# Tiles 0 and 1 of layer 0 taken through the slices of x together, and four smaller reorderings, in a two-layer hybrid encoder

## What is computed

```python
def hybrid_layer(x, ...):
    h = rms_norm(x, g)
    z = h @ w_in                       # 1024 -> 3712 columns, 29 tiles of 128
    # splits: aq ak av ag | bq bk bv bg | ca cb cg
    ya = neighbourhood_attention(aq, ak, av, rpb) * silu(ag)      # 4 heads, local window 8 x 16
    yb = dilated_attention(rotary(bq), rotary(bk), bv) * silu(bg) # 6 heads, three dilated windows
    yc = conformer_conv(ca, cb, ...) * silu(cg)                   # GLU, 31 taps, LayerNorm, pointwise
    return x + concat([ya, yb, yc]) @ w_out

h = x
for l in range(2):
    h = hybrid_layer(h, ...)
return rms_norm(h, final_g)
```

## Time and profile before

| | us |
|---|---|
| median of 3 runs | 562.41 |
| lowest and highest | 561.2, 562.55 |
| profiled execution | 561.84 |
| its span (first to last instruction) | 560.0 |

### The profile page before, as it was taken

The page is one execution under the profiler, slowest core; times in us unless marked ns, Lnnn a source line. Parts: engine busy times, 40 slices in busy tenths (PEclk is TensorE's granted clock), DMA queues, the critical chain, the costliest instruction groups (busy, mean ns, idle before and its releaser), DMA issues.

```text
span 560.0 us, 7459 instructions
## 1 busy us (share of the span) xinstructions
PE 543.9 (97%) x2716; PEld 419.8 (75%) x2716; DVE 368.7 (66%) x710; ACT 248.2 (44%) x465; POOL 213.0 (38%) x251
## 2 busy tenths in 40 slices
PE   7999999999999999999899999999999999999994
PEld 5788777676776787878777876767767687878883
DVE  6799999999743644612338998999994346453113
ACT  6333255454454454623332314544555445563422
POOL 0003456544354344326211325554436434243520
PEclk9999999999999999999999999999999999999998
DMA  8724677665576674999302349756567666379913
GB/s 267 258 76 114 163 167 172 153 136 121 124 169 134 148 156 89 252 272 198 119 0 95 95 109 228 170 117 143 137 132 166 147 151 153 76 170 222 189 36 150
DMA packets 30132, 83.64 MB, mean 149 GB/s; under 512 B 4240, under 2 KB 10256, under 8 KB 30096
## 3 DMA queue, kind: packets, MB, share of 16 engines
q0 software_dynamic: 17856, 61.09, 50.1%
q1 hardware_dynamic: 12240, 22.08, 11.9%
HBM read 77.91 MB, written 2.10 MB: 143 GB/s over the span
## 4 chain that ended last, share of the span: by engine, by line
PE 71%; DVE 11%; DMA 9%; issue 3%; ACT 1%; SPq 1%; POOL 1%; POOLq 0%; DVEq 0%; ACTq 0%
PE acc L438 19%; PE acc L440 17%; PE acc L439 17%; PE tp L511 5%; PE sc L497 5%; PE ob L539 4%; DMA w_lo<-w_in 3%; DVE w_lo L1123 2%; DMA w_hi<-w_out 2%; DMA w_lo<-w_out 2%; DVE acc L1044 2%; DVE act_lo L1145 1%; DVE y L1044 1%; DMA x<-xT 1%; PE misc L526 1%
## 5 line engine op out<-in xcount | busy, mean ns | idle before, releaser
L438 PE MATMUL acc<-act_hi,w_hi 128*128 128x512 f32 x576 | 235.4, 409 | 6.5 <-DVE act_lo L1145 3.8
L440 PE MATMUL acc<-act_lo,w_hi 128*128 128x512 f32 x576 | 225.3, 391 | 0.0
L439 PE MATMUL acc<-act_hi,w_lo 128*128 128x512 f32 x576 | 225.1, 391 | 0.0
L438 PEld LDWEIGHTS acc<-act_hi,w_hi 128*128 128x128 f32 x576 | 108.1, 188 | 43.6 <-issue 12.9
L874 POOL TENSOR_SCALAR prob<-prob,rden 128x512 f32<-128x512 f32 (+1 forms) x80 | 73.1, 913 | 154.5 <-DVE rden L1070 154.1
L440 PEld LDWEIGHTS acc<-act_lo,w_hi 128*128 128x128 f32 x576 | 108.1, 188 | 23.8
L439 PEld LDWEIGHTS acc<-act_hi,w_lo 128*128 128x128 f32 x576 | 108.4, 188 | 20.7 <-issue 1.0
L632 ACT ACTIVATE w_lo<-w_hi 128x1024 fp32r<-128x1024 f32 (+1 forms) x62 | 62.0, 1000 | 61.9 <-DMA w_hi<-w_out 36.4
L695 ACT ACTIVATE prob<-prob,nmx 128x512 f32<-128x512 f32 (+1 forms) x80 | 50.5, 632 | 53.5 <-DVE nmx L1064 53.5
L1044 DVE SCALAR_TENSOR_TENSOR y<-u,par,y 128x512 f32<-128x512 f32 x90 | 73.0, 811 | 0.0
L714 ACT ACTIVATE pT<-tp 128x512 f32<-128x512 f32 (+1 forms) x80 | 40.5, 507 | 72.8 <-PE tp L511 72.8
(11 more groups left out here) (119 smaller groups left out, 602.6 us busy)
## 6 DMA issues: line engine op xcount, KB each, us to landing
w_hi<-w_in POOLq DMA_DIRECT2D x40, 512.0 KB, 4.0
w_lo<-w_in POOLq DMA_DIRECT2D x40, 512.0 KB, 5.5
pT<-w_in SPq DMA_DIRECT2D x17, 512.0 KB, 4.6
w_hi<-w_out POOLq DMA_DIRECT2D x16, 512.0 KB, 6.8
w_lo<-w_out POOLq DMA_DIRECT2D x16, 512.0 KB, 6.8
bias<-nabias SPq DMA_DIRECT2D x32, 128.0 KB, 3.0
sq<-sq SPq DMA_DIRECT2D x48, 64.0 KB, 2.7
x<-xT SPq DMA_DIRECT2D x8, 256.0 KB, 5.5
```

Of the source, the lines that this page charges most:

```text
L438: nc.tensor.matmul(to[:, :], w_hi[:, slot, k, :], a_hi[:, k, :], start=i == 0, stop=False)
L439: nc.tensor.matmul(to[:, :], w_lo[:, slot, k, :], a_hi[:, k, :], start=False, stop=False)
L440: last = nc.tensor.matmul(to[:, :], w_hi[:, slot, k, :], a_lo[:, k, :], start=False, stop=i == K - 1)
```

## The change

1. Head of layer 0: tiles 0 and 1 go through the slices of x together, three products of each per slice (`FIRST = 2`, `PART_DUE`), and the raw chunks of both come in parts between the slices. Tiles 2 and 3 go to sc0 and sc1. The column sums of the norm stand behind half of tile 2 in layer 0 (before: behind tile 1), in layer 1 behind half of tile 1; the broadcast follows half a tile later.
2. GpSimd rotates the rotary half of a tile one step later in its queue.
3. The parameters of layer 1 are loaded ahead of its raw chunks.
4. The first four raw chunks of layer 1 each wait for one output tile, not all for the last product with the values.
5. Local attention: `scores` makes four units at a time (two blocks of queries for both heads) into the two halves of each score bank, every fourth unit.

```diff
-W0_PARTS = {0: (2, 5), 2: (0, 2), 4: (5, KD)}
-W0_DUE = [0, 3, 4, KD]
+FIRST = 2
+W_PARTS = [(2, 5), (0, 2), (5, KD)]
+N_PARTS = FIRST * len(W_PARTS)
+PART_DUE = [0, 0, 0, 1, 2, 2, 2, 2]
-COL_HALF, BC_HALF = 3, 4
+COL_HALF, BC_HALF = (4, 2), (5, 3)
...
+        def part_of(i):
+            return i % FIRST, slice(*W_PARTS[i // FIRST])
+        def score_at(g, b):
+            return 0 if g < DPAIRS else NKEY * (b % 2)
         def bank_of(c):
-            return sc[0] if c == 2 else acc[c % 2]
+            return sc[c % 2] if c in (2, 3) else acc[c % 2]
...
                 if l and c < RAW:
-                    sp.wait_ge(pv_done, PAIRS * l)
+                    sp.wait_ge(tile_done, N_CH * (l - 1) + N_IN + CT + c + 1)
...
             for i, k in enumerate(K_ORDER):
-                if i in W0_PARTS:
+                if i < N_PARTS:
                     load_first(i)
                 sp.dma_start(x[:, k, :], xT[:, k, :]).then_inc(x_in[k], 16)
-            load(0, 1)
             load(0, 2)
...
+                if l + 1 < DEPTH:
+                    sp.wait_ge(ylo_ready, KD * (l + 1))
+                    sp.dma_start(par[:, :], prm[l + 1]).then_inc(par_in, 16)
                 for c in range(N_IN, N_CH):
                     load_next(l, c)
-                if l + 1 < DEPTH:
-                    sp.wait_ge(ylo_ready, KD * (l + 1))
-                    sp.dma_start(par[:, :], prm[l + 1]).then_inc(par_in, 16)
...
-                    pe.wait_ge(acc_free, emptied(l, c - 2))
+                    pe.wait_ge(acc_free, emptied(l, c - (4 if c in (4, 5) else 2)))
...
-                    for i in range(len(W0_PARTS)):
-                        pe.wait_ge(w0_lo, i + 1)
-                        in_tile(0, 0, W0_DUE[i], W0_DUE[i + 1], ready=(xlo_ready, 0))
+                    for i in range(KD):
+                        for c in range(FIRST):
+                            pe.wait_ge(part_lo, FIRST * PART_DUE[i] + c + 1)
+                            products(c, act_hi, act_lo, i, i + 1, order=K_ORDER, ready=(xlo_ready, 0))
...
-                for half in range(2, 2 * PRE):
+                for half in range(2 * (1 if l else FIRST), 2 * PRE):
...
-                        if n % 2 == 0:
+                        if n % (2 if n < DUNITS else 4) == 0:
                             scores(l, n)
...
                     lo_next(l, c)
-                    if c < PRE - 1 and (r := rope_of(c)) is not None:
+                    if c and (r := rope_of(c - 1)) is not None:
                         rotate(l, r)
...
-                dve.wait_ge(s_ready, UNITS * l + n + 1)
+                dve.wait_ge(s_ready, UNITS * l + (n + 1 if g < DPAIRS else n // 4 * 4 + 3 + h))
...
-                    if l == 0 and i in W0_PARTS:
-                        dve.wait_ge(w0_hi, i // 2 + 1)
-                        weights_lo(0, 0, *W0_PARTS[i]).then_inc(w0_lo, 1)
+                    if l == 0 and i < N_PARTS:
+                        dve.wait_ge(part_hi, i + 1)
+                        weights_lo(0, i % FIRST, *W_PARTS[i // FIRST]).then_inc(part_lo, 1)
...
                 if l == 0:
-                    split_weights(0, 1)
                     for i in range(len(ADD_BETWEEN) + 1, KD):
                         first_sums(i)
                     split_weights(0, 2)
```

More of the change, by code:

```diff
@@ L205, in build @@
         lo_ready = sem("lo_ready")
[L206 to L208 removed]
+        part_in = [sem(f"part_in{i}") for i in range(N_PARTS)]
+        part_hi = sem("part_hi")
+        part_lo = sem("part_lo")
         xhi_ready = sem("xhi_ready")
@@ L371, in load_first @@
             def load_first(i):
-                part = slice(*W0_PARTS[i])
-                sp.dma_start(raw[:, 0, part, :], w_in[0, 0][:, part, :]).then_inc(w0_in[i // 2], 16)
+                c, part = part_of(i)
+                sp.dma_start(raw[:, c, part, :], w_in[0, c][:, part, :]).then_inc(part_in[i], 16)
             def swap(l, r):
@@ L420, in _ @@
                     sp.dma_start(par[:, :], prm[l + 1]).then_inc(par_in, 16)
+                for c in range(N_IN, N_CH):
+                    load_next(l, c)
             for a in range(QT):
@@ L491, in scores @@
                     pe.wait_ge(m_ready, UNITS * l + n)
[L493 to L500, removed]
+                for b in (range(b, b + 1) if g < DPAIRS else range(b, b + 2)):
+                    first, w = (0, SEQ) if g < DPAIRS else (ROWS * NA_LO[b], NKEY)
+                    at = score_at(g, b)
+                    for i, (q, k) in enumerate(((q_hi, k_hi), (q_lo, k_hi), (q_hi, k_lo))):
+                        for h in range(2):
+                            own = slice(HD * h, HD * (h + 1))
+                            last = nc.tensor.matmul(sc[h][:, at:at + w], q[own, g % 2, b * P:(b + 1) * P],
+                                                    k[own, g % 2, first:first + w], start=i == 0, stop=i == 2)
+                            if i == 2:
+                                last.then_inc(s_ready, 1)
             def turn(l, n):
@@ L748, in first_hi @@
             def first_hi(i):
-                part = slice(*W0_PARTS[i])
-                act.wait_ge(w0_in[i // 2], 16)
-                nc.scalar.activation(w_hi[:, 0, part, :], raw[:, 0, part, :], ACT.Copy).then_inc(w0_hi, 1)
+                c, part = part_of(i)
+                act.wait_ge(part_in[i], 16)
+                nc.scalar.activation(w_hi[:, c, part, :], raw[:, c, part, :], ACT.Copy).then_inc(part_hi, 1)
             for l in range(DEPTH):
@@ L1063, in maxima @@
                     add = bias[:, i % 2, :]
-                nc.vector.tensor_tensor_reduce(out=prob[:, n % PROBS, 0:w], in0=sc[n % 2][:, 0:w], in1=add, scale=-1.0,
+                at = score_at(g, b)
+                nc.vector.tensor_tensor_reduce(out=prob[:, n % PROBS, 0:w], in0=sc[n % 2][:, at:at + w], in1=add, scale=-1.0,
                                                scalar=3e38, op0=ALU.add, op1=ALU.min,
```

27 lines of the change are left out of this document (13 added, 14 removed).

## The result

The changed kernel takes 558.04 us (median of 4 executions, 557.46 to 558.76) against 562.38 of the kernel before on the same chip (4 executions): ratio 0.9928, 95% interval 0.991 to 0.9947, so -4.0 us. A second comparison on another chip gave 559.19 (9 executions) against 561.41 and 0.9963 (0.9945 to 0.998), -2.1 us. Predicted were 555.1 and -7.3: faster, as forecast. The first time lies inside the range of 553.0 to 559.0, the second just outside. A good 3 us of the gain are missing, by the second result 5.

A forecast was written before the change was run, and what follows sets the result against it. TensorE, busy 97% of the span, was taken as the bound. Terms +0.9 - 1.0 - 3.4 - 3.3 - 0.5 = -7.3 us took 561.84 to 554.5, plus 0.57 for the median: 555.1 us, range 553.0 to 559.0.

The forecast's parts named there:

- Head, +0.9: Start of layer 0: tiles 0 and 1 sharing x's slices would cost 0.9 us, bounds -0.5 and +2.2.
- the gap at 73.28: VectorE in layer 0: idle time assumed to absorb 0.6 of its 2.1 us delay before unit 2's transpose.
- a credit for the slow instruction of 2.23 at 74.07: VectorE in layer 0: an instruction of a kind that took 0.68 elsewhere might shorten, as GpSimd work beside it moved.
- Rotation, -1.0: GpSimd queue: rotating behind weight transfers would end the wait at layer 1's tile 10, at no cost; -1.0 us.
- Turn of layers, -3.4: From layer 0's last output tile to layer 1's tile 3: earlier parameters and a separate bank would remove idle, -3.4 us.
- Regrouping, -3.3: Local attention: eight score groups of twelve in place of sixteen of six save 0.41 us each for eight, -3.3 us.
- The rival by which it saves nothing: Local attention: the second query block could drain the array like a switch, so regrouping gains nothing; 558.4 us, chance 0.10.
- Raw chunks, -0.5: Output tiles of layer 0: spreading layer 1's raw chunks would end the 0.62 wait for chunk 34; -0.5 us.
- The rival "slower": Output tiles: raw chunks with transfers far below 253 GB/s make the kernel slower, 564 to 566 us; chance 0.04.
- on the bandwidth (558.2): Output tiles: raw chunks take the weights' DMA bandwidth, so 3.1 us are waited for; 558.2 us, chance 0.10.
- The rival on the clock, 0.06: Gap before layer 0's tile 2: TensorE falls to half clock, costing 5.5 us; 560.6 or 559.8 us, chance 0.06.

The follow-up runs named there:

- e5: Changed kernel with GpSimd's rotation of tile 8 moved behind the normalisation of unit 1; 556.05 us, ratio 0.9887 to the kernel before.
- e6: Changed kernel with the old head of layer 0 and the rotation of tile 8 behind unit 1's normalisation; 552.63 us, ratio 0.983 to the kernel before.
- e2: Changed kernel with the head of layer 0 as before; 554.91 us, ratio 0.9866 to the kernel before.
- e4: Changed kernel with layer 0's column sums directly behind tiles 0 and 1 and the broadcast behind half of tile 2; 555.23 us, ratio 0.9877.
- e3: Kernel before with only the rotation moved behind the next tile's weight transfers on GpSimd; 564.66 us, ratio 1.0037.
- e1: Changed kernel with the rotation back ahead of the next tile's low-half transfer on GpSimd; 557.47 us, ratio 0.9918 to the kernel before.
- e7: Kernel before with only the local scores regrouped, eight groups of twelve in place of sixteen of six; 559.14 us, ratio 0.9945.
- e8: Kernel before with only the turn of layers changed: parameters first, second score bank for tile 3, layer 1's sums and broadcast earlier; 557.97 us, ratio 0.9929.
- e12: The changed kernel run again with nothing edited, on another chip; 559.19 us, ratio 0.9963 to the kernel before.
- e9: Kernel before with only layer 1's four raw chunks each released by an output tile; 560.63 us, ratio 0.9987.
- e10: Kernel before with only layer 1's parameters moved ahead of its raw chunks on SP; 558.33 us, ratio 0.9941.
- e11: Changed kernel with layer 0's column sums and broadcast earlier and the rotation of tile 8 behind unit 1's normalisation; 552.65 us, ratio 0.9846.

## Why the prediction was right, and where it failed

**Head, +0.9: mis-sized, it costs 3.4** (e5 against e6; 3.5 by e2 against the changed kernel's first ratio), of which about 1 goes with the clock (2.4 to 2.6 in the two executions of e5 that kept it); either is above the bound of +2.2. TensorE's side went nearly as worked out: tiles 0 and 1 end near 19.4 (18.5 forecast), the split of chunk 2 ends at about 21.9 (21.6). The factor came at 29.58 (28.9). What failed is the conversion of VectorE's delay into TensorE's. I looked for the first late transpose at unit 2, with 0.20 us of slack, and passed over unit 1, which had none (norm done at 75.75, turn at 75.80); that is where TensorE waited 1.98, and unit 2's turn came at 84.17, not near 81. I let the gap at 73.28 swallow 0.6 and gave a credit for the slow instruction of 2.23 at 74.07; the same instruction was slow in the changed kernel too (1.76 at 76.93). And the swaps, which start when VectorE empties a tile, carry its delay on to GpSimd (2.7 at 57.75), where nothing absorbs it. e2 shows the rate: 3.0 us of factor are 3.2 us of TensorE. e4 shows the cause: with column sums and broadcast moved forward the loss is gone.

**Rotation, -1.0 and "costs nothing": wrong in sign.** I named what was queued behind the rotation, VectorE's add, and it did wait, 1.75. I did not ask what the earlier issues put on the DMA engines while the swaps run, nor who waits behind the *next* rotation: `norm` of unit 1. Alone the move costs 2.1 (e3); in the changed kernel it is worth about nothing (e1). The wait of 1.03 that I credited to it does go in e3, but it is no fixed cost: e7 and e8 do without it in the old order.

**Turn of layers, -3.4: right,** -3.38 in the same stretch, -4.0 in time (e8, -5.4 to -2.5).

**Regrouping, -3.3: right,** 2 x 1.57 = 3.1. The rival by which it saves nothing is out.

**Raw chunks, -0.5: right in kind,** 0.90 by the profile. I held back 0.2 and kept two rivals because 253 GB/s looked like a limit; it was not, the stretch moves 289 to 290. (The rival "slower" has a slip in its sum: to end 1.7 behind, a forecast of -7.3 has to lose 9.0 us, not 9.5. Nothing else hangs on it.)

Sum of the parts alone: +3.5 for the head, 0 for the rotation beside it, -4.0, -3.1, -0.7: -4.3, where the changed kernel measured -4.0 and -2.1. Each part is known to about 1 us, so the first agreement is closer than could be asked for, and the second leaves 2.2 us that no run explains. The 3.0 us between -7.3 and -4.3 are the head's 2.6 and the rotation's 1.0, less the 0.6 by which e8 measured more than 3.4 for the turn. That 558.04 lies inside the range is partly luck: the range reached that far for the rivals on the regrouping (558.4) and on the bandwidth (558.2), and neither came true.

**The rival on the clock, 0.06: the chance too low, the price too high.** The clock stayed up in the first trace and fell behind this gap in e5 and, with the sums in the gap, in e4; in e12 the mean clock of several executions is lower, but no trace says behind which gap. Where it fell behind this gap it cost 1.6 us (e5), not the 5.5 of a whole tile at 1.2 GHz; e5 shows it back at 1.00 before the tile's end. The Trainium skill, TensorE: Matmul & The Clock Gate, Part 1, puts an idle array back to half clock; e3 and e5 agree where it fell, and the changed kernel's traces show gaps as long behind which it stayed. Of the four traces with 2.41 or 2.42 us of idle ahead of tile 2 (the changed kernel, e1, e5, e12), the clock fell in one, e5.

## What to carry to other kernels

Before crediting a filled gap, follow the delayed factor through the engine that has no idle time, here VectorE at 31.79 of 32 us, and price it one to one. Where an order is moved in a queue, look one item further than what stood behind it, and at what it puts on the DMA engines meanwhile; a wait that vanishes is a gain only if the next wait on that path does not end at the same event. Then try the parts alone: of this change, three were good (-7.8 together) and the head took 3.5 of it away; with one rotation moved, and under the new head column sums and broadcast too, either head gives 552.6. And look at a wait in more than one trace before it is priced: the 1.03 at tile 10 was missing in two of five traces that have the rotation in the same place.

## What the runs showed of the hardware

- Four swaps of 32 partitions (64 KB each) took 3.9 us from first issue to the rotation's start with one weight transfer in flight (before), 7.0 with two more (the changed kernel), and 5.2 in e1, where SP's four issues alone took 3.68 instead of 2.41; what held SP there is open.
- Low halves of 512 KB issued at the same place in layer 1 landed after 7.1 to 7.2 us (e7, e8) or 7.9 to 8.6 (before, e9, e10); the cause was not tried.
- The granted clock fell from 1.00 to 0.54 or 0.50 behind idle stretches of 1.76 (e3), 2.41 (e5) and 3.66 us (e1), and in e4 behind 1.37 us and the short column sums. It stayed at 1.00 behind 2.42 and 1.98 (changed kernel), behind 2.41 (e1, ahead of tile 2) and in e11, which has e4's order there. The length of the gap alone did not decide it; a fall cost 1.5 to 1.6 us (e1, e3, e5) and 0.9 in e4 beside e11.
- The same GpSimd instruction (`norm`) over 128 x 512 took 0.69, 1.01 or 1.63 us in these traces; the cause was not tried.
